# Cross attention's output layer by token tiles, with the experts' norm, first query and first list for tile 0 inside the matmuls of tile 1

## The reference

```
h = h + mem_cross_attention(rms_norm(h, norm_xattn), mem_n, wq, wkv, wo)   # ends in o @ wo, 1024 x 1024
h = h + peer_ffn(rms_norm(h, norm_ffn), peer_wq, subkeys, u, v)
# peer_ffn, for each token t and each of 8 heads:
q = xt @ wq                                   # 2 queries of 128 per head
s = einsum('thpd,hpkd->thpk', q, subkeys)     # 128 scores for each of the 2 halves
s1, i1 = top_k(s[:, :, 0], 16); s2, i2 = top_k(s[:, :, 1], 16)
top_s, pos = top_k(s1[..., :, None] + s2[..., None, :], 16)     # 16 of 16384 experts
gate = softmax(top_s)
act = gelu(xb . u_tab[idx]);  out = sum(gate * act * v_tab[idx])
```

## Time and profile before

| | |
|---|---|
| median of 3 runs | 3109.48 us (3107.84 to 3110.67) |
| span of the profiled execution (first to last instruction) | 3096.7 us |
| PE busy | 2607.4 us, 84% |
| DVE busy | 2115.4 us, 68% |
| ACT busy | 1084.0 us, 35% |
| POOL busy | 590.1 us, 19% |
| indirect DMA | 536.90 MB of 810.85 MB |

### The profile page before, as it was taken

The page is one execution under the profiler, slowest core; times in us unless marked ns, Lnnn a source line. Parts: engine busy times, 40 slices in busy tenths (PEclk is TensorE's granted clock), DMA queues, the critical chain, the costliest instruction groups (busy, mean ns, idle before and its releaser), DMA issues. The chain is left out here.

```text
span 3096.7 us, 36048 instructions
## 1 busy us (share of the span) xinstructions
PE 2607.4 (84%) x13122; PEld 1899.7 (61%) x13122; DVE 2115.4 (68%) x4127; ACT 1084.0 (35%) x1947; POOL 590.1 (19%) x547
## 2 busy tenths in 40 slices
PE   8988999998999899899787667668999787766665
PEld 7957997895899797797543222225888653222222
DVE  6467664647665566553899888866663689888875
ACT  4355443436444365444212111113654221112111
POOL 0000000000000000000345444440000254444442
PEclk9999999999999999999999888988999898888888
DMA  6422553551355433244899999997434799999996
GB/s 262 168 87 96 180 191 134 198 191 55 123 181 186 163 120 136 82 163 162 346 427 419 427 426 427 426 427 300 160 109 157 285 421 426 426 427 427 426 427 282
DMA packets 112498, 810.85 MB, mean 262 GB/s; under 512 B 12736, under 2 KB 12736, under 8 KB 14272
## 3 DMA queue, kind: packets, MB, share of 16 engines
q0 software_dynamic: 73728, 536.90, 41.4%
q1 hardware_dynamic: 38592, 271.63, 24.5%
HBM read 807.44 MB, written 1.05 MB: 261 GB/s over the span
## 5 line engine op out<-in xcount | busy, mean ns | idle before, releaser
L3214 PE MATMUL ps<-arena 128*128 128x512 f32 x912 | 514.8, 715 | 244.2 <-ACT arena L3138 244.2
L162 DVE TENSOR_TENSOR ring_low<-ring,parts 128x2048 fp32r<-128x2048 f32 x216 | 492.3, 2291 | 333.0 <-ACT parts L155 329.4
L453 PE MATMUL ps<-parts,parts 128*128 128x256 f32 x2528 | 568.8, 283 | 13.5 <-DVE ring_low L162 10.1
L3214 PEld LDWEIGHTS ps<-arena 128*128 128x128 f32 x912 | 200.3, 229 | 546.8 <-ACT arena L3138 324.5
L453 PE MATMUL ps<-parts,ring_low 128*128 128x256 f32 x1824 | 511.8, 281 | 0.0
L155 ACT ACTIVATE parts<-ring 128x2048 fp32r<-128x2048 f32 x216 | 410.7, 1913 | 281.8 <-PE ps L461 109.8
L461 PE MATMUL ps<-parts,parts 128*128 128x512 f32 x1344 | 439.2, 396 | 7.5 <-DVE ring_low L162 5.4
L453 PEld LDWEIGHTS ps<-parts,parts 128*128 128x128 f32 x2528 | 427.7, 189 | 16.4 <-issue 10.8
L2991 POOL DMA_INDIRECT arena<-in_experts,stage_index x276 | 314.8, 1140 | 549.3 <-PE ps L3214 251.1
L3214 PE MATMUL ps<-ring,arena 128*128 128x512 f32 x616 | 322.8, 663 | 113.3 <-ACT arena L3138 113.3
L3013 DVE CUSTOM_DVE_ANT_0 arena<-arena 128x1024 f32<-128x1024 f32 x276 | 333.5, 1226 | 94.2 <-DMA arena<-in_experts,stage_index 91.4
(11 more groups left out here) (480 smaller groups left out, 2966.1 us busy)
## 6 DMA issues: line engine op xcount, KB each, us to landing
ring<-in_stream SPq DMA_DIRECT2D x249, 1024.0 KB, 4.8
arena<-in_experts,stage_index POOLq DMA_INDIRECT x276, 22.7
ring<-in_experts,stage_index POOLq DMA_INDIRECT x236, 24.5
gain_row<-in_gain_rows SPq DMA_DIRECT2D x4, 512.0 KB, 5.8
arena<-in_mem SPq DMA_DIRECT2D x2, 1024.0 KB, 5.7
arena<-in_stream SPq DMA_DIRECT2D x2, 1024.0 KB, 8.2
par<-in_params SPq DMA_DIRECT2D x4, 386.0 KB, 3.0
x<-in_x SPq DMA_DIRECT2D x1, 1024.0 KB, 4.9
```

Of the source, the lines that this page charges most:

```text
L162: dve.tensor_tensor(k.ring_low[v % SLOTS], whole, self.high[:, c % self.HIGH_SLOTS, :].bitcast(F32), ALU.subtract).then_inc(self.ph.sem("c ...
L453: last = pe.matmul(self.ps[:, 2 * pair + f // 2, (f % 2) * T:(f % 2 + 1) * T], w[:, f * P:(f + 1) * P], x[:, k, :], start=(k == 0 and i == ...
L3214: last = pe.matmul(k.ps[:, bank + n, :], diag[:, s % ROWS, :], rows[row_of[s]][:, D + n * BLK:D + (n + 1) * BLK], start=(s % SLOTS_PER_TOK ...
```

## The change

The output layer runs over tiles outside and halves inside: tile 0 whole, then tile 1 whole. For that all four chunks must be split early, so chunk 3's high part has a place of its own (`split.home`, in the room of the scores of tile 1); `o_high` moves to the late part of the arena, so that pairs 6 and 7 may be filled only after the whole output layer. Between the matmuls of the output layer PE now runs, at fixed places (tile, half, block): the turns of tile 0, the first two queries of tile 0, and their scores. `TileNorm` takes the place of `LateNorm`: a mean and root for each tile, the squares all on ACT. DVE adds x by tile and half, runs `first_eight` before it adds tile 1, and releases the ring slots of chunks 1 and 3 when it takes tile 1's halves.

```diff
-        def outputs(n):
-            pair = (lo.group0 + n) % 2
...
+        def outputs(m):
+            pe.wait_ge(ph.sem("out_split"), m + 1)
+            toks = slice(m * P, (m + 1) * P)
+            for n in range(2):
...
                 for kt in range(KT):
+                    if (m, n, kt) in expert_early:
+                        expert_early[m, n, kt](pe)
...
-            last.then_inc(ph.sem("pair_done"), 1)
+                last.then_inc(ph.sem("first_tile_out" if m == 0 else "pair_done"), 1)
...
-        if c >= self.HIGH_SLOTS:
+        if c >= self.HIGH_SLOTS and v not in self.home:
...
+    split.home[lo.chunk0 + 3], _ = k.at_parts(SCORES_FROM + 16 * PE_KEYS, CHUNK)
...
             elif pair >= 6:
-                pool.wait_ge(norm.x_added, 2)
+                pool.wait_ge(ph.sem("pair_done"), lo.group0 + 2)
...
     def sync(sp):
         if layer + 1 < DEPTH:
-            sp.wait_ge(norm.split_ready, KT)
+            sp.wait_ge(norm.split_ready, MT * KT)
...
     def vector(dve, link):
-        add_block(k, dve, ph, lo, 0, norm.x_added)
-        add_block(k, dve, ph, lo, 1, norm.x_added)
-        norm.statistics(dve, link)
...
+        def second_added(n):
+            pair, free = k.take(dve, ph, lo, n)
...
+        first_added(0)
         link(dve.memset(z.index, 0.0))
+        norm.begin_mean(dve, link)
+        first_added(1)
+        norm.mean(dve, link, 0)
+        norm.finish(dve, link, 0)
         dve.wait_ge(ph.sem("iota_ready"), 1)
+        z.first_eight(dve, ph, link, staged)
+        second_added(0)
+        z.keys(dve, link, 0, (0, 1), have=8)
+        second_added(1)
+        z.part_of_routing(dve, ph, link, 0, 2, staged)
+        norm.mean(dve, link, 1)
+        z.part_of_routing(dve, ph, link, 0, 3, staged)
+        norm.finish(dve, link, 1)
+        for i in range(4, 7):
             z.part_of_routing(dve, ph, link, 0, i, staged)
         dve.wait_ge(ph.sem("gain_loaded"), 16)
+        gained(0)
         z.part_of_routing(dve, ph, link, 0, 7, staged)
+        gained(1)
...
-        norm.make_whole(act, 0)
-        norm.make_whole(act, 1)
+        norm.half_squares(act, 0)
+        norm.make_whole(act, 0, 0)
+        norm.half_squares(act, 1)
+        norm.make_whole(act, 0, 1)
+        norm.root(act, 0)
+        n_copies = [0]
+        first_tile_query()
+        act.wait_ge(norm.root_ready, 1)
+        copy_scores(0, [0, 1])
         norm.squares(act)
+        norm.make_whole(act, 1, 0)
+        norm.make_whole(act, 1, 1)
+        norm.root(act, 1)
+        exponentials(0)
         rest_of_query()
...
+    def turn_first(pe):
+        norm.turn(pe, 0, 0)
+    def turn_and_ask(pe):
+        norm.turn(pe, 0, 1)
+        k.linear_piece(pe, ph, lq, k.hT, 0, range(0, 4), range(0, 2), norm, None, toks=first_tile, first=False)
+    def ask(pe):
+        k.linear_piece(pe, ph, lq, k.hT, 0, range(4, KT), range(0, 2), norm, "query_parts", toks=first_tile, first=False)
+    def first_scores(pe):
+        pe.wait_ge(ph.sem("subkeys_loaded"), 16)
+        pe.wait_ge(ph.sem("queries_ready"), 1)
+        key_scores(pe, 0, range(0, 2))
+    early = {(0, 1, 4): turn_first, (1, 0, 2): turn_and_ask, (1, 0, 5): ask, (1, 0, 7): first_scores}
...
-        queries(0, ks=range(0, 3), fs=range(0, 2), done=None, toks=first_tile)
-        norm.turn(pe, 1)
-        queries(0, ks=range(3, KT), fs=range(0, 2), done="query_parts", toks=first_tile)
-        pe.wait_ge(ph.sem("subkeys_loaded"), 16)
-        some_scores(0, range(0, 2), 1)
-        queries(0, fs=range(2, 4), done="query_parts", frees=False)
+        pe.wait_ge(ph.sem("scores_copied"), 1)
+        norm.turn(pe, 1, 0)
+        norm.turn(pe, 1, 1)
+        queries(0, fs=range(2, 4), done="query_parts", frees=False, after=KT)
         some_scores(0, range(2, 4), 2)
-        queries(0, fs=range(0, 2), toks=second_tile, frees=True, first=False)
+        queries(0, fs=range(0, 2), toks=second_tile, frees=True, first=False, after=KT)
         some_scores(1, range(0, 4), 3)
```

More of the change, by code:

```diff
@@ L2558, in cross_attention @@
     spare, _ = k.at(a, 2, D)
[L2559 removed]
+    a += KT * T
     probs, a = k.at(a, MT, 4, T)
@@ L2630, in tensor @@
         values(1)
-        outputs(0)
-        outputs(1)
+        for m in range(MT):
+            outputs(m)
     def scalar(act):
@@ L2858, in part_of_routing @@
         n = UNITS[u][2]
[L2859 to L2862, removed]
+        if i == 0:
             dve.wait_ge(ph.sem("scores_copied"), SCORES_FOR[u])
@@ L3184, in scalar, with key_scores @@
             root(1)
+    first_tile, second_tile = slice(0, P), slice(P, T)
+    def key_scores(pe, m, js):
+        for j in js:
+            last = pe.matmul(k.ps[:, 4 + m, (j % 4) * P:(j % 4 + 1) * P], z.qT[:, j % 4, m * P:(m + 1) * P],
+                             z.subkeys[:, j * P:(j + 1) * P], start=True, stop=True)
+        last.then_inc(ph.sem("scores_done"), 1)
+    def turn_first(pe):
[10 more added lines that the diff above has]
+    early = {(0, 1, 4): turn_first, (1, 0, 2): turn_and_ask, (1, 0, 5): ask, (1, 0, 7): first_scores}
     def tensor(pe):
@@ L3192, in some_scores @@
             pe.wait_ge(ph.sem("queries_ready"), n_ready)
[L3193 to L3198, removed]
+            pe.wait_ge(ph.sem("scores_copied"), n_scores[0] - 1 if n_scores[0] <= 3 else n_scores[0] - 2)
+            key_scores(pe, m, js)
         def scores(n):
@@ L3236, in tensor @@
                 scores((4, 14, 26).index(g) + 1)
-    return Part(sync, tensor, scalar, vector, pool, loads)
+    return Part(sync, tensor, scalar, vector, pool, loads, early)
 def diags_by(g):
@@ L3261, in attend_phase @@
                         junk=(spare[:, 0, 0:D], spare[:, 1, 0:D]), tag="mem_", stat=32)
-        norm = LateNorm(ph, k.x, k.p2("norm_ffn"), (k.hT, None), (z.scores[:, 0, 0:8, :].rearrange("p a b -> p (a b)"), z.xt[:, 1, :]),
+        norm = TileNorm(ph, k.x, k.p2("norm_ffn"), k.hT, [z.scores[:, m, 0:8, :].rearrange("p a b -> p (a b)") for m in range(MT)],
                         "expert_", stat=16)
-        norm.from_ = z.late_start
         out = mixer_out(k, ph, split, lin, sources, gains, memory, mem_norm)
         expert = experts(k, ph, lq, lins[3], z, norm, layer)
-        attend = cross_attention(k, ph, split, lins, lq, memory, mem_norm, (mem_high, mem_low), norm, expert.loads)
+        attend = cross_attention(k, ph, split, lins, lq, memory, mem_norm, (mem_high, mem_low), z.late_start, expert.loads, expert.early)
         with k.engines(ph) as block:
```

108 lines of the change are left out of this document (80 added, 28 removed).

## The result

The changed kernel takes 3087.86 us (median of 4 runs, 3086.61 to 3088.8), the kernel before 3108.98 us beside it (4 runs, 3107.84 to 3110.67): ratio 0.9933, 95% interval 0.9921 to 0.9945. That is 21.1 us less. The profiled execution of the changed kernel has a span of 3086.8 us and a time of 3088.53 us, 1.7 us above its span.

A forecast was written before the change was run, and what follows sets the result against it. The DMA engines, once full, bound the expert stages. Earlier first list, minus loads among the gathers, plus the closed gap gave 6.1 and 7.0 us: 3109.5 - 13.1 = 3096.4 us, range 3089 to 3106.5 (8 in 10).

The forecast's parts named there:

- Part A: Before the first gather: the first list of experts comes earlier, by 9.4 us in layer 0 and 8.9 in layer 1.
- Rivals 3 and 4: Output layer: PE waits for inputs, 3106.4 us, chance 0.08; or a wait drops the clock, 3119.4 us, chance 0.05.
- Part B: First gathers: ring loads and parameters pushed among them cost 8.3 us in layer 0, 7.4 us in layer 1.
- rival 1: Expert stages: loads cost nothing, since something other than DMA sets the pace; 28.8 us gained, 3080.7 us; chance 0.10.
- Part C: Eleventh gather: the DMA engines' gap there closes, gaining 5.0 us in layer 0 and 5.5 us in layer 1.
- rival 2: Eleventh gather: it comes after the engines ran dry, so the gap stays; 2.6 us gained, 3106.9 us; chance 0.12.
- The sum: Both layers: 6.1 us in layer 0 and 7.0 us in layer 1, 13.1 us off the span of 3096.7 us.
- The median of the runs lies 12.8 us above the span and moves with it: Whole kernel: the 12.8 us between profiled span and median stay fixed, so the median becomes 3096.4 us.

The follow-up runs named there:

- loads_twice: The changed kernel with SyncE's last two loads of each output layer each made twice: 3093.77 us, ratio 0.9955 to the kernel before.
- before_fourth: The kernel before, unchanged, run once more to catch its trace where it takes 3108 us: 3109.56 us, ratio 0.9999.
- chain_only_2: Repeat of the changed kernel with VectorE adding tile 1's second half before sorting keys and ScalarE copying tile 1 before the squares: 3086.82 us, ratio 0.9921.

## Why the prediction was wrong

**Part A** held: 10.3 and 9.7 us measured for 9.4 and 8.9. Scores began 20.5 us after S (1463.46 - 1442.92) where I had 21.3; the waits and entries I charged 0.7 us for cost next to nothing. Rivals 3 and 4 are out: no wait stands ahead of the early steps, and the clock stayed at 1.00. The Trainium skill's page "TensorE: Matmul & The Clock Gate", section "Part 4: PE-mode transpose", says that transposes do not count as activity for the clock as matmuls do. No effect of that shows here: eight transposes between matmuls, and no lower clock.

**Part B** held in kind: most of the loads' bytes are paid. Its size was not measured by itself, it is what the table leaves over. With total gain = A + C - B, B is 10.3 + 3.1 - 6.8 = 6.6 us and 9.7 + 4.5 - 8.1 = 6.1, for 8.3 and 7.4, near its lower bound. loads_twice, where 9.8 us of such bytes cost 5.9 to 8.5 us, speaks against rival 1.

**Part C** was 5.0 - 1.9 = 3.1 us and 5.5 - 1.0 = 4.5, for 5.0 and 5.5. The refill came 7.3 and 8.6 us earlier relative to S, and in time: S + 56.0 is 1497.1 on the time axis of the kernel before, where I wanted it before 1498. The gap at the eleventh gather closed, with the DMA engines full to S + 68 (less than 0.2 us lost from S + 40 to there). What is lost, 1.9 and 1.0 us, lies from S + 68 to S + 84, behind the gathers that wait for the next buffers. I had left those out. It is not rival 2, which has the eleventh gather too late.

**The sum**, 13.1 us, stands against 11.8 us between the two first traces, and 13.8 and 12.0 us in the two comparisons in which the kernel before took 3099 and 3098 us.

**The step that failed** is "The median of the runs lies 12.8 us above the span and moves with it". Of the 12.8 us only 1.7 or 1.8 are what every execution here has above its own span. The other 11 were a second form of the kernel before, which its profiled execution did not have: TensorE's last signal of the first query group comes 3.2 to 4.9 us late, in both layers, and the eleventh gather with it. (The three runs themselves left no trace; that they had this form is read from before_fourth, which takes the same time.) These 11 us did not move with the kernel. The change puts that signal 16.6 us and more after the first gather, outside the time in which it is held up, and takes the exponentials out from behind it. So the change gains 12 to 14 us where the kernel before is in its short form, and 21 us where it has the late signal. That the sum meets the first of these so closely is in part luck: its terms are off by 0.8 to 1.9 us in each layer, A and B in its favour and C against it. Had I asked why a profiled execution should be 12.8 us shorter than three runs that agree within 3 us, I would have seen that the sum lacked a second mechanism, and that its range had to be open downwards.

What stays open: what holds TensorE's signals up in some comparisons and not in others of the same program. It is not the chip, since two chips showed both. The recording of the executions is a rival that no run here rules out, since records are lost in just those comparisons. Open too is whether the products or only their signal come late; the trace models the ends of matmuls. I have not tried to move the gathers against a fixed signal. And the changed kernel took 3087.86 us in the comparison with the longer time and 3085.32 and 3086.45 in the others, for which I have no cause.

## What to carry to other kernels

A distance between a profile's span and the median of the runs is a quantity to be explained before anything is added to it: in this kernel 1.7 us of it is constant and the rest was an effect the change removed. Where transfers and the chain that returns their buffers are both nearly the limit, bytes added cost more than half of their time here (5.9 to 8.5 us for 9.8), bytes moved earlier alone bring nothing measurable, and four edits on both together bring 3 to 5 us; the chain alone was shortened in one layer only, for 1 us at most. A wait costs what hangs behind it in the engine's program order: the same late signal cost the kernel before 11 us and chain_only_2 nothing. Other work put between the matmuls of a layer cost no more than its own time where its inputs were there, and brought a whole stage forward by 10 us.

## What the hardware showed that I had not expected

In some comparisons the signal of a TensorE matmul that starts 6.6 to 9.3 us after the first of eight gathers arrives only 11.4 to 11.7 us after that gather, whichever engine waits, and one in the midst of the group at 9.3 to 11.5 us. Signals recorded up to 5.0 us after the gather, or from matmuls that start 11.5 us after it or later, are prompt (0.31 to 0.42 us). The traces of just these comparisons lack 1.8 to 2.5% of the records of a DMA's change of a semaphore, most densely where the gathers of a stage begin. The same program on the same chip took 3099 us in one comparison and 3110 us in another, all its runs alike each time. And the releaser named beside such a wait was a load that had long landed, or "remote": a releaser that can't be right is itself a hint that a signal was late.
